# The second expert's rows added by the gathering transfer, in a two-layer mLSTM and dilated-attention trunk with routed experts

## The reference

```python
ybuf = lax.map(run, (xbuf.reshape(n_blocks, MOE_BLOCK, d), block_e)).reshape(n_blocks * MOE_BLOCK, d)
y = ybuf[dest] * flat_w[order][:, None].astype(t.dtype)
out = jnp.zeros((n_tok, d), t.dtype).at[tok].add(y)
...
x = layer_norm(ALPHA * x + (1.0 + g2) * y, ln_g[l, 1], ln_b[l, 1])
if l == N_A_LAYERS - 1:
    kv = (x @ b_w_kv).reshape(bsz, s, 2, B_GROUPS, B_HEADS, B_HEAD_DIM)
    k_sh = rope(kv[:, :, 0], positions)
```

## Time and profile before

| | us |
|---|---|
| median of 3 runs | 4369.67 (4368.86 to 4376.23) |
| the profiled execution: its own time | 4371.31 |
| the profiled execution: its span | 4369.3 |
| PE busy, share of the span | 3823.4, 88% |
| DVE busy | 2186.8, 50% |
| ACT busy | 1441.8, 33% |
| POOL busy | 500.5, 11% |
| mean DMA rate over the span | 217 GB/s |

### The profile page before, as it was taken

How to read it: one execution, slowest core, us unless ns; L and a number is a source line. 1 busy time by engine, 2 the same in 40 slices (tenths; PEclk the granted TensorE clock), 3 DMA queues, 4 the chain that set the end, 5 groups by cost and what they waited for, 6 DMA issues and landing times. The chain is left out here.

```text
span 4369.3 us, 54002 instructions
## 1 busy us (share of the span) xinstructions
PE 3823.4 (88%) x17360; PEld 2828.0 (65%) x17360; DVE 2186.8 (50%) x4789; ACT 1441.8 (33%) x3067; POOL 500.5 (11%) x457
## 2 busy tenths in 40 slices
PE   5999795979959999985998998989996959999990
PEld 3888674868736555554886776868885735555550
DVE  4222314865445555555764333225436845555557
ACT  2222202632233333332222113216565533333334
POOL 0010000000001111104540002331000001111103
PEclk8999897989969999997999999999998969999995
DMA  7343312643159999986646533225455349999988
GB/s 251 125 134 116 127 68 82 208 146 114 65 183 389 390 389 390 389 302 217 181 149 209 171 122 110 79 71 171 131 157 169 132 157 387 392 388 392 388 325 322
DMA packets 651484, 949.10 MB, mean 217 GB/s; under 512 B 31941, under 2 KB 522133, under 8 KB 630085
## 3 DMA queue, kind: packets, MB, share of 16 engines
q1 hardware_dynamic: 596358, 770.90, 51.3%
q0 software_dynamic: 27360, 99.63, 5.9%
q10 hardware_dynamic: 27632, 76.87, 4.4%
HBM read 745.38 MB, written 201.93 MB: 217 GB/s over the span
## 5 line engine op out<-in xcount | busy, mean ns | idle before, releaser
L1529 PE MATMUL ex_gu<-ex_wgu,ex_hT 128*128 128x512 f32 x2016 | 910.8, 595 | 6.9 <-ACT ex_hT L1584 6.9
L1529 PEld LDWEIGHTS ex_gu<-ex_wgu,ex_hT 128*128 128x128 f32 x2016 | 374.8, 191 | 383.8 <-issue 369.6
L1661 DVE TENSOR_TENSOR ex_wds<-ex_wd,ex_wds 128x2048 fp32r<-128x2048 f32 x126 | 288.9, 2293 | 247.0 <-ACT ex_wds L1591 247.0
L1547 PE MATMUL ex_acc<-ex_wds,ex_aT 128*128 128x512 f32 x1512 | 384.7, 403 | 7.7 <-DVE ex_aT L1657 7.7
L2238 PE MATMUL pvo_mm<-pvo_ws,pvo_hT 128*128 128x512 f32 x1536 | 361.8, 395 | 8.7 <-POOL pvo_hT L2389 8.7
L2238 PEld LDWEIGHTS pvo_mm<-pvo_ws,pvo_hT 128*128 128x128 f32 x1536 | 289.0, 190 | 72.7 <-POOL pvo_hT L2389 9.6
L1606 ACT ACTIVATE ex_sg<-ex_gu 128x256 f32<-128x256 f32 x126 | 48.3, 383 | 829.6 <-PE ex_gu L1529 829.6
L1547 PEld LDWEIGHTS ex_acc<-ex_wds,ex_aT 128*128 128x128 f32 x1512 | 277.4, 190 | 65.2 <-DVE ex_aT L1657 8.1
L978 PE MATMUL am_acc<-am_ws,am_yT 128*128 128x512 f32 x1152 | 295.1, 411 | 21.2 <-issue 15.0
L2238 PE MATMUL pq_mm<-pq_ws,pq_hT 128*128 128x512 f32 x1152 | 269.4, 394 | 21.3 <-POOL pq_hT L2389 20.5
L2238 PE MATMUL pv_mm<-pv_ws,pv_hT 128*128 128x512 f32 x1152 | 269.3, 394 | 16.3 <-DVE pv_hT L2362 13.0
(11 more groups left out here) (346 smaller groups left out, 5416.1 us busy)
## 6 DMA issues: line engine op xcount, KB each, us to landing
ex_wgu<-in_moe_w_gate_dram SPq DMA_DIRECT2D x126, 1024.0 KB, 8.8
ex_wgu<-in_moe_w_up_dram SPq DMA_DIRECT2D x126, 1024.0 KB, 12.1
ex_wd<-in_moe_w_down_dram SPq DMA_DIRECT2D x126, 1024.0 KB
ybuf_scratch<-ex_y ACTq DMA_DIRECT2D x126, 512.0 KB
pv_m_w<-in_ada_w_dram SPq DMA_DIRECT2D x16, 1536.0 KB, 8.1
pvo_r_w<-in_ada_w_dram SPq DMA_DIRECT2D x32, 512.0 KB
vo_scratch<-pvo_vo SPq DMA_DIRECT2D x16, 1024.0 KB
x_scratch<-am_x SPq DMA_DIRECT2D x32, 512.0 KB, 3.0
```

The costliest lines, as they stand in the source:

```text
L1529: ins = nc.tensor.matmul(gu[j][:, :, :], hT[:, j, k, :], wgu[:, jw, k, :, :], start=(k == 0), stop=(k == KD - 1))
L1547: ins = nc.tensor.matmul(acc[half][:, :], aT[:, hi_a, k, :], wds[:, j, hi_w, k, half * CH:(half + 1) * CH], start=(k == 0 and n == 0), sto ...
L1661: nc.vector.tensor_tensor(wds[:, j, 1, :, :], wd[:, j, :, :], wds[:, j, 0, :, :], ALU.subtract).then_inc(wlo_ready, 1)
```

## The change

Each tile's `y` is now one slot of 128 x 1024 instead of two halves. The first expert's rows are gathered into it as before. When they have landed, POOL issues a second indirect transfer with `compute_op=ALU.add` to the same slot: the DMA engines read the second expert's row and add it to what the slot holds. No engine adds the two any more. DVE waits for the second transfer. In the k projection the second transfer (`add_second`) stands where POOL's sum stood, four tiles ahead. In the last phase POOL's order is gather two tiles ahead, then `add_second`; POOL now waits in `add_second` for the first transfer's landing, and its wait for a free slot is on `z_ready`, which DVE gives after `total`. The other edits are names and semaphore counts. The number of bytes read from `ybuf` is the same.

```diff
--- before.py
+++ after.py
@@ -1863,15 +1863,16 @@
         self.norm = ph.sb("norm", [P, 2, D])
         self.dest, self.destb = ph.sb("dest", [P, NT, 2], I32), ph.sb("destb", [P, 2, 2], I32)
         self.x1 = ph.sb("x1", [P, 2, D])
-        self.y = ph.sb("y", [P, 2, 2, D])
+        self.y = ph.sb("y", [P, 2, D])
         self.z = self.x1
         self.x2 = ph.sb("x2", [P, 2, D])
         self.stats, self.mv, self.rstd = ph.sb("stats", [P, 2, 6]), ph.sb("mv", [P, 2, 2]), ph.sb("rstd", [P, 2, 3])
         self.dest_in = ph.sem("dest_in")
-        self.cb_in, self.ysum_ready, self.y_used, self.v_ready, self.std_ready, self.x2_ready, self.waited = (
-            ph.sem(s) for s in ("cb_in", "ysum_ready", "y_used", "v_ready", "std_ready", "x2_ready", "cb_waited"))
+        self.pool_waited = ph.sem("cb_pool_waited")
+        self.cb_in, self.y_used, self.v_ready, self.std_ready, self.x2_ready, self.waited = (
+            ph.sem(s) for s in ("cb_in", "y_used", "v_ready", "std_ready", "x2_ready", "cb_waited"))
         self.x1_in, self.stored = ([ph.sem(f"{n}{j}") for j in range(2)] for n in ("x1_in", "stored"))
-        self.y_in = d["pool_dma"](f"cb{l}")
+        self.y_in, self.ysum_in = d["pool_dma"](f"cb{l}")[0:2], d["pool_dma"](f"cb{l}")[2:4]
 
     def sync_dest(self, sp):
         sp.dma_start(self.dest[:, :, :].rearrange("p c j -> p (c j)"), self.d["dest"]).then_inc(self.dest_in, 16)
@@ -1905,15 +1906,16 @@
             wait_from(pool, self.y_used, c - 1)
             nc.gpsimd.tensor_copy(self.destb[:, j, :], self.dest[:, ds(c, 1), :])
             pool.drain()
-            for n in range(2):
-                nc.gpsimd.indirect_dma_start(out=self.y[:, j, n, :], out_offset=None, in_=self.d["ybuf"],
-                                             in_offset=bass.IndirectOffsetOnAxis(ap=self.destb[:, j, n:n + 1], axis=0)).then_inc(self.y_in[j], 16)
-
-        def sum_experts(c, j):
-            pool.wait_ge(self.y_in[j], 16 * (c - j) + 32)
-            nc.gpsimd.tensor_tensor(self.y[:, j, 0, :], self.y[:, j, 0, :], self.y[:, j, 1, :], ALU.add).then_inc(self.ysum_ready, 1)
-
-        return [(sum_experts, self.lead + 1), (gather, self.lead + 2)]
+            nc.gpsimd.indirect_dma_start(out=self.y[:, j, :], out_offset=None, in_=self.d["ybuf"],
+                                         in_offset=bass.IndirectOffsetOnAxis(ap=self.destb[:, j, 0:1], axis=0)).then_inc(self.y_in[j], 16)
+
+        def add_second(c, j):
+            pool.wait_ge(self.y_in[j], 8 * (c - j) + 16)
+            settle(pool, self.pool_waited)
+            nc.gpsimd.indirect_dma_start(out=self.y[:, j, :], out_offset=None, in_=self.d["ybuf"],
+                                         in_offset=bass.IndirectOffsetOnAxis(ap=self.destb[:, j, 1:2], axis=0), compute_op=ALU.add).then_inc(self.ysum_in[j], 16)
+
+        return [(add_second, self.lead + 1), (gather, self.lead + 2)]
 
     def scalar_stages(self, act):
         def root(c, j):
@@ -1931,8 +1933,8 @@
         def total(c, j):
 
             dve.wait_ge(self.x1_in[j], 8 * (c - j) + 16)
-            dve.wait_ge(self.ysum_ready, c + 1)
-            v.scalar_tensor_tensor(z[:, j, :], self.x1[:, j, :], ALPHA, self.y[:, j, 0, :], ALU.mult, ALU.add)
+            dve.wait_ge(self.ysum_in[j], 8 * (c - j) + 16)
+            v.scalar_tensor_tensor(z[:, j, :], self.x1[:, j, :], ALPHA, self.y[:, j, :], ALU.mult, ALU.add)
             dve.drain().then_inc(self.y_used, 1)
             for half in range(2):
                 v.bn_stats(stats[:, half, :], z[:, j, half * CH:(half + 1) * CH])
@@ -1970,17 +1972,17 @@
         norm = ph.sb("norm", [P, 2, D])
         dest = ph.sb("dest", [P, NT, 2], I32)
         x1 = ph.sb("x1", [P, RB, D])
-        y = ph.sb("y", [P, RB, 2, D])
+        y = ph.sb("y", [P, RB, D])
         z = ph.sb("z", [P, 2, D])
         x2 = ph.sb("x2", [P, 2, D])
         spare = ph.sb("spare", [P, D])
         eps = ph.sb("eps", [P, 1])
         sums = ph.sb("sums", [P, 2, 4])
         rstd = ph.sb("rstd", [P, 2, 1])
-        dest_in, norm_in, eps_ready, y_used, z_ready, std_ready, x2_ready = (
-            ph.sem(s) for s in ("dest_in", "norm_in", "eps_ready", "y_used", "z_ready", "std_ready", "x2_ready"))
+        dest_in, norm_in, eps_ready, z_ready, std_ready, x2_ready = (
+            ph.sem(s) for s in ("dest_in", "norm_in", "eps_ready", "z_ready", "std_ready", "x2_ready"))
         x1_in, stored = [ph.sem(f"x1_in{j}") for j in range(RB)], [ph.sem(f"stored{j}") for j in range(2)]
-        y_in = d["pool_dma"](f"cb{l}")
+        y_in, ysum_in = d["pool_dma"](f"cb{l}")[0:RB], d["pool_dma"](f"cb{l}")[RB:2 * RB]
 
         with nc.Block() as block:
             @block.sync
@@ -2011,12 +2013,16 @@
 
                 def gather(c, j):
                     if c >= RB:
-                        pool.wait_ge(y_used, c - RB + 1)
-                    for n in range(2):
-                        nc.gpsimd.indirect_dma_start(out=y[:, c % RB, n, :], out_offset=None, in_=d["ybuf"],
-                                                     in_offset=bass.IndirectOffsetOnAxis(ap=dest[:, c, n:n + 1], axis=0)).then_inc(y_in[c % RB], 16)
-
-                straight(pool, [(gather, 0)])
+                        pool.wait_ge(z_ready, c - RB + 1)
+                    nc.gpsimd.indirect_dma_start(out=y[:, c % RB, :], out_offset=None, in_=d["ybuf"],
+                                                 in_offset=bass.IndirectOffsetOnAxis(ap=dest[:, c, 0:1], axis=0)).then_inc(y_in[c % RB], 16)
+
+                def add_second(c, j):
+                    pool.wait_ge(y_in[c % RB], 16 * (c // RB) + 16)
+                    nc.gpsimd.indirect_dma_start(out=y[:, c % RB, :], out_offset=None, in_=d["ybuf"],
+                                                 in_offset=bass.IndirectOffsetOnAxis(ap=dest[:, c, 1:2], axis=0), compute_op=ALU.add).then_inc(ysum_in[c % RB], 16)
+
+                straight(pool, [(gather, 2), (add_second, 0)])
 
             @block.scalar
             def _(act):
@@ -2041,11 +2047,10 @@
 
                 def total(c, j):
 
-                    dve.wait_ge(y_in[c % RB], 32 * (c // RB) + 32)
-                    v.tensor_tensor(z[:, j, :], y[:, c % RB, 0, :], y[:, c % RB, 1, :], ALU.add).then_inc(y_used, 1)
-                    dve.drain()
+                    dve.wait_ge(ysum_in[c % RB], 16 * (c // RB) + 16)
                     dve.wait_ge(x1_in[c % RB], 16 * (c // RB) + 16)
-                    v.scalar_tensor_tensor(z[:, j, :], x1[:, c % RB, :], ALPHA, z[:, j, :], ALU.mult, ALU.add).then_inc(z_ready, 1)
+                    v.scalar_tensor_tensor(z[:, j, :], x1[:, c % RB, :], ALPHA, y[:, c % RB, :], ALU.mult, ALU.add)
+                    dve.drain().then_inc(z_ready, 1)
 
                 def normalise(c, j):
                     if c == 0:
@@ -2636,7 +2641,7 @@
 def trunk(nc, d):
 
 
-    pool_dma = {n: [nc.semaphore(f"{n}_pool_dma{j}").__enter__() for j in range(k)] for n, k in (("ex0", 2), ("ex1", 2), ("cb0", 2), ("cb1", 4))}
+    pool_dma = {n: [nc.semaphore(f"{n}_pool_dma{j}").__enter__() for j in range(k)] for n, k in (("ex0", 2), ("ex1", 2), ("cb0", 4), ("cb1", 8))}
     d["pool_dma"] = pool_dma.__getitem__
     fw = FirstWeights(nc)
     modulation(nc, d, fw)
```

## The result

| | before | changed |
|---|---|---|
| median, us | 4370.6 (4368.86 to 4376.23, 4 runs) | 4395.48 (4394.36 to 4395.97, 4 runs) |
| profiled execution, own time / span | 4371.31 / 4369.3 | 4395.86 / 4393.5 |
| k projection, load of the indices to first v matmul | 374.9 | 381.0 |
| last phase, load of the indices to the end | 103.8 | 124.5 |

The changed kernel is slower, ratio 1.0053 (95% interval 1.0038 to 1.0068). Of the 24.2 us between the two profiled spans 20.7 lie in the last phase and 6.1 in the k projection. What remains, -2.6, lies in parts that the change does not touch and is taken as scatter: the stretch ahead of the k projection is 4.3 us shorter, the rest between the two places 1.7 longer.

A forecast was written before the change was run, and what follows sets the result against it. The prediction took DVE to bound the last phase at 5.26 us per tile, with DMA at 5.19 close behind. +18 us there and -3 in the k projection gave +15, 4384.7 us on the median, range 4363 to 4406.

The forecast's parts named there:

- The bound read before the change: Last phase: DVE sets the pace at 5.26 us per tile, DMA second at 5.19 us, 0.07 us behind.
- The addition in flight, taken as a second read: Last phase: the second transfer costs engines twice a gather, 2.62 MB per tile, 6.49 us at 404 GB/s.
- The chain of waits: Last phase: total, gather issue, then second transfer's landing span two tile periods, 2P = 3.6 + L = 11.9, P = 5.95 us.
- L: Last phase: the second transfer's time from issue to landing, 7.0 us plus 1.3 for its own second half.
- idle DMA engines: Last phase: the sign that the chain of waits is the bound; otherwise the DMA share should stay near 1.0.
- the end's 3 us: Last phase: the last two second transfers land in 4.2 to 5.1 us instead of 7.0, so 3 us off.
- The start: Last phase: the addition's result for tile 1 comes 4.7 us later, 6 us with doubled reads.
- The k projection: Its start: gathers and rotated parts go out earlier and PE's 3.78 us wait goes, -3 us with doubled reads.
- the second transfers hidden: k projection: second transfers, issued four tiles ahead with 18.6 us per tile, cost nothing; uncovered, each would cost 5 us.
- A: Rival, chance 0.35: the addition in flight costs no more than a plain gather, L = 7.0, P = 5.3; 4365 us.
- B: Rival, chance 0.08: as A, but the chain does not bind, P = 5.19, k projection -8 us; 4360 us.
- C: Rival, chance 0.15: last phase's second transfers land like its slowest gather, L = 12.3, P = 7.95; 4407.7 us.

The follow-up runs named there:

- e1: The change in the last phase alone, with the k projection of the kernel before: 4389.49 us, ratio 1.0048 to the kernel before.
- e2: The change in the k projection alone, with the last phase of the kernel before: 4372.2 us, ratio 1.0007 to the kernel before.
- e10: e4 with a plain second gather that overwrites the first, so no addition of the experts in the last phase: 4365.64 us, ratio 0.999.
- e4: e1 with last-phase rings of 8 slots instead of 4 and the first gather four tiles ahead instead of two: 4383.37 us, ratio 1.0036.
- e3: e1 with the last phase's second transfer a plain gather that overwrites the first, every wait kept: 4380.95 us, ratio 1.0027.
- e5: e2 with the next tile's index copy and its drain made before the second transfer is issued: 4357.51 us, ratio 0.9969.
- e7: Kernel before, POOL's k projection stages reordered: rotated parts first, then the experts' sum, then the gathers: 4362.1 us, ratio 0.9982.
- e6: e2 with the k projection's second transfer a plain gather that overwrites the first: 4365.72 us, ratio 0.999.

## Why the prediction was right, and where it was off

*Direction and range held:* slower, inside 4363 to 4406, by 24.9 us where 15 were forecast. By the profiles 9.1 of the missing 10 lie in the k projection and 2.7 in the last phase, with the scatter elsewhere taking 2 back; by e1 and e2, each against its own runs of before, it is 1.8 in the last phase and 5.5 in the k projection, and 2.6 us of the full change's 24.9 are in neither.

*The bound read before the change* held: the kernel had DVE at 5.26 us per tile and DMA close behind it. But the 404 GB/s that I took for the engines' limit were the rate at DVE's pace. e10, where DVE does no addition, runs at 4.98 us and 420 GB/s, so the second bound was 0.28 us behind, not 0.07.

*The addition in flight, taken as a second read:* right in its price. I worked with 2.62 MB per tile and 6.49 us; e4 gives 6.30. Collectives: The Full Stack in the Trainium skill ("The bandwidth ceiling: the fold count and why AG ≠ RS ≠ AR") says of the reducing step of a ReduceScatter ring that it pays for its second source read; that agrees with the 1.32 us per tile between e10 and e4, though the page states it for such a ring and not for a gather. That the price is a read, and not something else that costs as much, no run here shows.

*The chain of waits:* right in form, 2P = 3.6 + L, wrong in the size of L. I took 8.3 us and so let DMA bind; measured are 10.1, which gives P = 6.85, and the trace shows 6.91 from tile 4 to tile 12 and 6.98 from tile 5 to tile 13. So the chain binds and DMA stands 0.6 to 0.7 us behind. The sign that I had set for this, idle DMA engines, did not show it: the share reads 1.01 at 304 GB/s here and 1.05 at 332 in e4, so a share of one does not say that the engines could not do more. The mis-sized term is landing time: I carried over the 7.0 us of a phase in which DVE spaced the issues evenly. In the closed circle the issues bunch, and e3 has 9.8 us at a lower load. The estimate of 3.2 us by the Trainium skill's page DMA: Bandwidth & Descriptors ("Anatomy of one DMA — SWDGE (gpsimd) path") is further off. That half of the 7.0 us was queueing was no reading of a row: against the 4.2 to 5.1 us of the k projection's steady part it is 2 to 3. In the sum, 14 intervals less the end's 3 us were to be 87.9 us; from tile 1 (4290.91) to tile 15 (4382.48) it is 91.6. The start came 5.2 us later, within the phase, against 6. Together +20.7 for +18. That the two lie so close is in part luck. With the binding wait at its true size the 14 intervals are 6 us longer than I had them, and the end gave back 5.4 us (the last two intervals are 4.22 and 4.21) where I took off 3.

*The k projection:* this step failed. In the trace the k projection became longer, which I had named as a sign of a wrong forecast. I wrote that the gather of tile 4 could go out near 2019 and PE's wait would go. The second transfer did go out at 2020.19, but the gather only at 2030.15, because the drain between them lasts until the transfer has landed. I also called the second transfers hidden; those of tiles 2 and 3 held DVE for 16.2 us in all. In place of -3 the trace has +6.1, and the runs +2.5 (e2) and +5.1 (the full change less e1), which is small beside the scatter of that stretch; that the 3 us of gain did not come is clear, how much was lost is not. The sign of what I named as gain was right for the order without that drain: e5 gains 13.4 us. The row that could have warned me stood in the prediction: PE waited for POOL's drain, which ended at 2048.35, 3 us after the rotated parts and within 0.3 us of the landing of a gather issued at 2040.54. I read it as the parts being late, not as the drain waiting for a transfer.

*The rivals:* A needed both an addition for nothing and L = 7.0; neither is so. B's k projection gain of 8 us exists in e5 and e7, by another order of POOL's work. C's 12.3 us landing did not come, though 10.1 is half-way to it from my 8.3, and C had the binding wait right.

## What to carry to other kernels

Moving work from an engine to the transfer pays where the transfer has slack in time and in bandwidth, and not where the DMA engines are the second bound: first find the next bound, then the length of the new chain of waits, and take landing times from a stretch whose issues are as bunched as they will be. When two limits lie close together and one is removed in an experiment, the loss hardly moves; only the version without both shows that nothing else is there. On POOL, look at what is issued ahead of every drain.

## What the runs showed of the hardware

A drain on POOL behind an issued indirect transfer lasts until that transfer has landed, as far as the rows show: median 5.90 us behind the accumulating transfer, 4.18 behind a plain one, 0.42 when the order puts none right before it. The instruction behind the drain starts 0.7 to 0.9 us after the landing at all 15 tiles of the changed kernel and all 15 of e6, with landings from 4.2 to 10.5 us. Whether it waits for the landing itself or for something that ends with it stays open.

An accumulating indirect transfer of 128 x 1024 float32 takes POOL 1.56 us to issue in the k projection's steady part, where a plain one takes 0.96 (e6) at the same place. It takes 9.3 us to land there, the plain one at the same place 7.7; the first gathers, issued at another point of the tile, land in 4.3 us in both kernels, so the point of issue counts for more than the addition. In DMA time, at full engines, it costs two plain ones: 1.32 us on top of 1.25.

The busy share of the DMA engines is no measure of what is left in them: 1.01 went with 304 GB/s in the changed kernel, 1.03 with 420 in e10.
